# A pool mixer, a conv/LRU mixer and a PEER expert layer on one core: reordering the conditioning sums, the gating products and the transposes of the first norm

## The reference, cut to what matters

```
# first block: pool mixer (DEPTH = 1, so only this mixer runs)
h = x @ w_in;  u, z = h[:, :2048], h[:, 2048:]
per group g of 512 channels, window w = 2, 4, 8, 16:
    m[g] = moving_mean_w(u[g]) - u[g]
    m[g] = m[g] @ w_grp[g]
y = (m * scale * silu(z)) @ w_out
x = layer_norm(2**0.25 * x + y)
# second block, conditioned on c
ada = silu(c) @ w_ada + b_ada            # 6 * 1024 values: shift, scale, gate, twice
h = rmsnorm(x) * (1 + scale1) + shift1
z = h @ w_in2                            # gate_b, gate_c, xa, xr, gr
y = [gated short convolution ; gated linear recurrence], normalized per head
x = x + gate1 * (y @ w_out2)
h = rmsnorm(x) * (1 + scale2) + shift2
x = x + gate2 * peer(h)                  # per token 8 heads x 16 experts, gathered rows of 2 x 1024
out = rmsnorm(x) * final_g
```

## Time and profile before

| | |
|---|---|
| time, median of 3 runs | 1865.74 us (1862.46 to 1865.97) |
| time of the profiled execution | 1871.87 us |
| its span | 1870.0 us (1.9 us lie around the span) |
| TensorE busy / VectorE busy / ScalarE busy / POOL busy | 1598.8 / 1520.7 / 343.5 / 805.3 us |
| granted TensorE clock, mean of the span | 0.978 |
| HBM read | 621.06 MB |

### The profile page before, as it was taken

One profiled execution on the slowest core, in us unless ns is written; L12 is line 12 of the kernel. 1 busy time (PEld: TensorE's weight loads), 2 busy tenths in 40 slices (PEclk: granted clock), 3 DMA queues, 4 the chain that ended last, 5 costly groups with the idle time before them and its releaser, 6 DMA issues.

```text
span 1870.0 us, 19089 instructions
## 1 busy us (share of the span) xinstructions
PE 1598.8 (85%) x4856; PEld 830.0 (44%) x4856; DVE 1520.7 (81%) x3533; ACT 343.5 (18%) x955; POOL 805.3 (43%) x559
## 2 busy tenths in 40 slices
PE   7989999799988888888878888887888888788886
PEld 6768788677643333333333333332333333333332
DVE  5777786578768888888878888887888888788887
ACT  5223233254321101100111010011101001110101
POOL 1000000000016666666546666654666755456662
PEclk9999999899998999999999999999999999999999
DMA  8555463142229999999999999999999999999996
GB/s 304 180 203 179 168 229 144 40 175 85 90 77 391 421 421 421 421 422 421 422 404 412 422 418 422 422 410 383 413 422 422 422 421 416 387 416 421 422 422 255
DMA packets 93678, 623.89 MB, mean 334 GB/s; under 512 B 11440, under 2 KB 11440, under 8 KB 24240
## 3 DMA queue, kind: packets, MB, share of 16 engines
q0 software_dynamic: 78912, 570.46, 74.4%
q1 hardware_dynamic: 14704, 52.74, 7.7%
HBM read 621.06 MB, written 2.10 MB: 333 GB/s over the span
## 4 chain that ended last, share of the span: by engine, by line
DMA 41%; PE 30%; DVE 13%; issue 7%; POOL 5%; DVEq 3%; ACT 1%; POOLq 0%; ACTq 0%; SPq 0%
DMA arena<-in_experts,idx 38%; PE ps L625 9%; PE ps L413 5%; PE ps L414 5%; PE ps L415 5%; DVE arena L1336 5%; POOL arena L402 5%; PE ps L545 3%; DMA arena<-in_w_ada 2%; DVE arena L944 1%; DVE arena L1360 1%; PE ps L576 1%; DMA arena<-in_w_in 1%; DVE arena L1119 1%; DVE arena L1228 1%
## 5 line engine op out<-in xcount | busy, mean ns | idle before, releaser
L625 PE MATMUL ps<-arena 128*128 128x512 f32 x2048 | 1010.3, 623 | 225.3 <-DVE arena L1360 221.6
L402 POOL DMA_INDIRECT arena<-in_experts,idx x512 | 784.1, 1531 | 714.9 <-issue 389.3
L625 PEld LDWEIGHTS ps<-arena 128*128 128x128 f32 x2048 | 357.9, 192 | 829.4 <-DVE arena L1360 554.2
L1336 DVE CUSTOM_DVE_ANT_0 arena<-arena,ada 128x1024 f32<-128x1024 f32 x512 | 627.1, 1225 | 108.2 <-DMA arena<-in_experts,idx 89.9
L849 ACT ACTIVATE arena<-arena 128x1 f32<-128x1 f32 x512 | 103.9, 203 | 1135.1 <-DVE arena L1336 1135.1
L1360 DVE TENSOR_SCALAR arena<-ident,arena 128x128 f32<-128x128 f32 x512 | 171.0, 334 | 1.6 <-ACT arena L849 1.6
L365 POOL DMA_DIRECT2D arena<-in_w_ada x24 | 12.9, 538 | 247.4 <-DVE arena L944 237.3
L413 PE MATMUL ps<-xT_hl,w_hl 128*128 128x512 f32 x192 | 79.2, 412 | 9.4 <-DVE xT_hl L908 9.4
L903 DVE TENSOR_TENSOR w_hl<-arena,w_hl 128x1024 fp32r<-128x1024 f32 x47 | 57.4, 1221 | 30.0 <-ACT w_hl L653 29.9
L414 PE MATMUL ps<-xT_hl,w_hl 128*128 128x512 f32 x192 | 76.8, 400 | 0.0
L415 PE MATMUL ps<-xT_hl,w_hl 128*128 128x512 f32 x192 | 76.7, 400 | 0.0
(11 more groups left out here) (228 smaller groups left out, 1654.6 us busy)
## 6 DMA issues: line engine op xcount, KB each, us to landing
arena<-in_w_ada POOLq DMA_DIRECT2D x24, 1024.0 KB, 5.2
arena<-in_w_in SPq DMA_DIRECT2D x44, 512.0 KB, 3.3
arena<-in_experts,idx POOLq DMA_INDIRECT x512
arena<-in_w_out SPq DMA_DIRECT2D x14, 512.0 KB, 5.4
lnw<-in_w_in SPq DMA_DIRECT2D x8, 512.0 KB, 4.6
arena<-in_w_grp POOLq DMA_DIRECT2D x4, 1024.0 KB, 7.1
arena<-in_w_out SPq DMA_DIRECT2D x1, 4096.0 KB, 12.7
arena<-in_w_q SPq DMA_DIRECT2D x1, 4096.0 KB, 13.4
```

The source lines that it names most:

```text
L402: nc.gpsimd.indirect_dma_start(ring[:, n % RING, :], None, experts, bass.IndirectOffsetOnAxis(ap=idx[:, e, n:n + 1], axis=0)).then_inc(arr ...
L625: last = mm(ps[half][:, :], lhsT=diag[:, n % RING, :], rhs=ring[:, n % RING, DM + half * T:DM + (half + 1) * T], start=(e == 0 and n == 0) ...
L1336: nc.vector.tensor_tensor_reduce(out=urow, in0=urow, in1=h2cur, scale=1.0, scalar=0.0, op0=ALU.mult, op1=ALU.add, accum_out=dots[:, e, n:n ...
```

## The change

The sums over partitions of a group are taken inside the next group, after its second chunk (for the last group: after the second chunk of the output product). VectorE's order at a group's end becomes: one half, two gating products, one half, two gating products, remaining halves; in the last group all four gating products, then the remaining half. `ada_add` moves from the first to the third step of the next group (in the output product from chunks 0 and 1 to chunks 3 and 4). The transposes of h1 for tiles 0 and 1 are put between the first and the second chunk of the output tiles 2 and 3. The half blocks of the second mixer's first product go: the block is done once, for 512 tokens, and waits for the last tile's low parts in two steps.

```
@@ -414,16 +414,17 @@
                 mm(dst, lhsT=lhs[0], rhs=rhs[1], start=False, stop=False)
                 return mm(dst, lhsT=lhs[1], rhs=rhs[0], start=False, stop=final)
 
-            def chunk_mm(dst, w, x_hl, tok=slice(0, T), x_ready=None):
+            def chunk_mm(dst, w, x_hl, x_ready=None, halves=None):
 
                 for k in range(KD):
                     if x_ready is not None:
                         pe.wait_ge(x_ready, k + 1)
+                    if halves is not None and k % (KD // 2) == 0:
+                        pe.wait_ge(halves, 2 * NT - 1 + k // (KD // 2))
                     c = slice(k * P, (k + 1) * P)
-                    last = split_mm(dst[:, tok], (w[:, 0, c], w[:, 1, c]), (x_hl[:, k, 0, tok], x_hl[:, k, 1, tok]),
+                    last = split_mm(dst[:, :], (w[:, 0, c], w[:, 1, c]), (x_hl[:, k, 0, :], x_hl[:, k, 1, :]),
                                     k == 0, k == KD - 1)
-                if tok.stop == T:
-                    last.then_inc(w_mm, 1)
+                last.then_inc(w_mm, 1)
 
 
             pe.wait_ge(consts, 5)
@@ -434,6 +435,12 @@
                 pe.wait_ge(ada_acc, 2 * p + 2)
                 mm(ada_bank(p)[:, :], lhsT=ones[:, :], rhs=adaacc[:, p % ADA_ACC, :], start=True,
                    stop=True).then_inc(acc_mm, 1)
+
+            def sum_pairs(g):
+
+                for i in range(PAIRS[g]):
+                    pe.wait_ge(z_ready, GC * g + i + 1)
+                    sum_ada(PAIR0[g] + i)
 
             for g in range(NG):
                 for s in range(2 * GC):
@@ -445,6 +452,8 @@
                         if s - GC < PAIRS[g - 1]:
                             pe.wait_ge(ada_added, PAIR0[g - 1] + s - GC + 1)
                     chunk_mm(ps[s], hl_of(8 * g + s), xT_hl, x_ready=x_lo if g == 0 and s == 0 else None)
+                    if g and s == 1:
+                        sum_pairs(g - 1)
                 for d in range(GC):
                     for c in range(GC):
                         if d == 0:
@@ -453,9 +462,6 @@
                         last = split_mm(ps[d][:, :], (wgrp_hi[:, c, f], wgrp_lo[:, c, f]),
                                         (pooled_hi[:, c, :], pooled_lo[:, c, :]), c == 0, c == GC - 1)
                     last.then_inc(grp_mm, 1)
-                for i in range(PAIRS[g]):
-                    pe.wait_ge(z_ready, GC * g + i + 1)
-                    sum_ada(PAIR0[g] + i)
 
 
             def wout_mm(c, t, first, final):
@@ -483,12 +489,8 @@
                         pe.wait_ge(yin_ready, NKP - NT + t + 1)
                     last = wout_mm(c, t, c % 8 == 0, c == 7)
                 last.then_inc(w_mm, 1)
-            for t in range(NT):
-                for c in range(NWO - NRES, NWO):
-                    if t == 0:
-                        pe.wait_ge(lo_ready, NIN + c + 1)
-                    last = wout_mm(c, t, False, c == NWO - 1)
-                last.then_inc(yout_mm, 1)
+                if c == 1:
+                    sum_pairs(NG - 1)
 
             def transpose_h1(t):
                 pe.wait_ge(h1_ready, t + 1)
@@ -498,14 +500,15 @@
                                                h1tmp[:, t % 2, k * P:(k + 1) * P], ident[:, :])
                 last.then_inc(h1_tr, 1)
 
-            for t in range(NT - 1):
-                transpose_h1(t)
-
-            first = FIRST2
-            pe.wait_ge(h1_lo, 4)
-            for s in (XR, GR):
-                pe.wait_ge(lo_ready, first + s + 1)
-                chunk_mm(ps[s], hl_of(first + s), h1T_hl, slice(0, T // 2))
+            for t in range(NT):
+                for c in range(NWO - NRES, NWO):
+                    if t == 0:
+                        pe.wait_ge(lo_ready, NIN + c + 1)
+                    last = wout_mm(c, t, False, c == NWO - 1)
+                    if t >= 2 and c == NWO - NRES:
+                        transpose_h1(t - 2)
+                last.then_inc(yout_mm, 1)
+            transpose_h1(NT - 2)
             transpose_h1(NT - 1)
 
 
@@ -517,7 +520,6 @@
                 mm(ps[7][:, :], lhsT=headmean[:, :], rhs=(sqb if n % 2 == 0 else sqa)[:, 0:T],
                    start=True, stop=True).then_inc(norm_mm, 1)
 
-            pe.wait_ge(h1_lo, 2 * NT)
             read_by = {XR: xr_copied, GR: gg_ready, GCT: gc_copied, XA: v_ready, GB: ya_ready}
             for j in range(NJ):
                 for s in range(5):
@@ -525,7 +527,7 @@
                     pe.wait_ge(lo_ready, n + 1)
                     if j:
                         pe.wait_ge(read_by[s], j)
-                    chunk_mm(ps[s], hl_of(n), h1T_hl, slice(T // 2 if n < first + 2 else 0, T))
+                    chunk_mm(ps[s], hl_of(n), h1T_hl, halves=h1_lo if n == FIRST2 else None)
                     if j and s == XR:
                         head_means(2 * j - 2)
                     if j and s == GR:
@@ -728,12 +730,11 @@
                                    ps[4 * b + t][:, :].rearrange("p (k f) -> p k f", k=4)).then_inc(h1_hi, 1)
 
             for t in range(NT):
-                if t == NT - 1:
-                    h1_hi_part(0)
-                    h1_hi_part(1)
                 act.wait_ge(var_ready, t + 1)
                 nc.scalar.activation(stats[:, 13:14], stats[:, 13:14], ACT.Sqrt,
                                      bias=stats[:, 16:17]).then_inc(root_ready, 1)
+                if t >= 2:
+                    h1_hi_part(t - 2)
                 root_of_squares(xres[:, t, :], junk1, t + 1)
             for t in range(NT - 2, NT):
                 h1_hi_part(t)
@@ -1001,7 +1002,7 @@
                 b = 2 * PAIR0[g]
                 for s in range(GC):
                     lo_part(8 * g + s + 2)
-                    if s == 0 and g:
+                    if s == 2 and g:
                         for p in range(PAIR0[g - 1], PAIR0[g]):
                             ada_add(p)
                     if s:
@@ -1026,19 +1027,28 @@
                 if g == NG - 1:
                     for c in range(4):
                         yin_lo_part(c)
+                if g < NG - 1:
+                    ada_half(b)
+                    gated(g, 0)
+                    gated(g, 1)
+                    ada_half(b + 1)
+                    b += 2
+                    gated(g, 2)
+                    gated(g, 3)
+                else:
+                    for d in range(GC):
+                        gated(g, d)
                 while b < 2 * PAIR0[g + 1]:
                     ada_half(b)
                     b += 1
-                for d in range(GC):
-                    gated(g, d)
 
             for c in range(8):
                 lo_part(NIN + c + 2)
                 if c < 6:
                     yin_lo_part(2 * c + 4)
                     yin_lo_part(2 * c + 5)
-                if c < 2:
-                    ada_add(PAIR0[NG - 1] + c)
+                if c in (3, 4):
+                    ada_add(PAIR0[NG - 1] + c - 3)
                 if c < 4:
                     ada_half(2 * PAIR0[NG] + c)
             ada_add(NPAIR - 2)
@@ -1086,8 +1096,6 @@
                 nc.vector.bn_aggr(stats[:, 12:14],
                                   lnst[:, t, :].rearrange("p (a b) -> p a b", a=2)).then_inc(var_ready, 1)
                 dve.drain()
-                if t == NT - 1:
-                    h1_lo_part(0)
                 stt(row, row, stats[:, 12:13], lnw[:, 0, :], ALU.subtract, ALU.mult)
                 inverse_root(13, 2 * t + 1)
                 stt(row, row, stats[:, 13:14], lnw[:, 1, :], ALU.mult, ALU.add).then_inc(row_ready, 1)
@@ -1095,11 +1103,11 @@
                 if t >= 2:
                     dve.wait_ge(h1_tr, t - 1)
                 tt(h1, row, ada[:, 1, :], ALU.mult)
-                if t == NT - 1:
-                    h1_lo_part(1)
                 inverse_root(14, 2 * t + 2)
                 stt(h1, h1, stats[:, 14:15], ada[:, 0, :], ALU.mult, ALU.add).then_inc(h1_ready, 1)
-            for t in range(NT - 2, NT):
+                if t == 2:
+                    h1_lo_part(0)
+            for t in range(1, NT):
                 h1_lo_part(t)
```

29 lines of the change are left out of this document (12 added, 17 removed).

## The result

The changed kernel takes 1849.2 us (median of 4 runs, 1847.89 to 1849.7) against 1865.86 us before (median of 4): ratio 0.9904, 95% interval 0.989 to 0.9919. A later comparison with more runs gives 1849.34 against 1865.73, ratio 0.9911 (0.9897 to 0.9925). So 16.4 to 16.7 us are gained; 21.8 were forecast. The measured time lies inside the stated range (1839.5 to 1855) and 0.2 us above the forecast's own (1840 to 1849). The two profiled executions, 1871.87 and 1847.89 us, lie 24.0 us apart, 7 us more than the medians. Where these 7 us come from is the main question of the experiments.

The account below looks back on a forecast made before the run. The gather fills the DMA engines from 560 us on; before it TensorE paces, so the gain is an earlier gather start. 1.0 + 8.1 + 7.7 + 5.0 = 21.8 us off the 1865.74 median gives about 1844.0 us; range 1839.5 to 1855.

Parts of the forecast that it names:

- Part 1: Ends of the first three groups: TensorE's waits and restarts go, gaining 1.0, 8.1 and 7.7 us.
- the gain does not depend on that: The profiled execution lay 6.1 us over the median; the full 21.8 us was therefore taken off the median too.
- rival A: VectorE falls behind in the third and fourth groups and output product: 12 us of gain lost, 1856 us; chance 0.12.
- B: The first norm gives nothing, its first two blocks perhaps all at the lower clock: 1851 us; chance 0.16.
- Do the waits only move?: Group ends: waits do not reappear in the next group; slack 4.0 us in the second, 3 us in the third; cost nothing.
- Part 2: First norm, up to the gate matmuls: transposes inside tiles 2 and 3 and whole blocks bring these 5.0 us forward.
- C: Sums inside the next group: a half over 4 us late holds the group and starts it cold; some 1879 us; chance 0.03.
- D: Start of the gather: set by the mixer's loads or the ScalarE chain, so no change, about 1865 us; chance 0.04.

Follow-up runs that it names:

- first profile of before: The kernel before the change, unchanged, as first profiled: profiled execution 1871.87 us, median of runs 1865.86 us.
- second profile: A repeat profile of an unchanged kernel: the kernel before took 1866.59 us (median), the changed kernel 1849.34 us.
- norm part: Only the norm edits (transposes inside output tiles 2 and 3, whole blocks), against the kernel before: 1860.24 us, ratio 0.9971.

## Why the prediction was right, and where its sum was off

- **Part 1, the groups.** The mechanism is right in each point: banks 0 and 1 gated before the product ends, sums at full speed inside the next group, no wait for a sum or a bank anywhere (ten sums run after second chunks; the prediction counted eight, those of the groups). The term is oversized. It was 16.8 us; against the first profile of before the last sums moved by 16.5 us, but in that execution the clock had fallen at both ends, in the second profile at the third group's end alone. Against the second it is 11.0 to 11.5 us, and by the runs 9.9. The step that failed is the sentence that "the gain does not depend on that": the profiled execution lay 6.1 us over the median, and 5.1 of these were in the group ends, which the change removes. Priced from the second profile by the same count, the three ends give an estimate of 0.8 + 3.9 + 7.0 = 11.7 us instead of 16.8 (6.3 and 9.4 less 2.4 each, and 1.0 less the 0.2 by which the first group's wait was shorter); that alone is the 5.1 us between forecast and result. The other differences are small: 1.8 us less by the runs than by this count, 0.8 more in the norm, and 0.7 to 1.0 that both parts together give over their sum. That the time still lies in the stated range is owed to the width that the rivals A and B gave it: it is 0.2 us outside the forecast's own range.
- **Do the waits only move?** No, as forecast. The slack was 6.7 and 4.8 us instead of 4.0 and 3 in the first profile, since the last load but one was in by 119.9 instead of 122.6. In the second profile the same load came at 122.2, and the slack was 4.7 and 6.0 us: the 4.0 was a fair figure, and the landing decides it. Of the last load's 7.55 us, which the prediction read as its length, 3.9 were spent behind the load before it.
- **VectorE falls behind (rival A).** It did not: no wait for it in the third or fourth group. Only with 9.2 us of added work does a part of this appear.
- **Part 2, the norm.** 5.0 forecast, 5.6 to 5.7 by the profiles (93.4 to 87.7, or 93.1 to 87.5 for the part alone), 5.8 by the runs. The fourth row was complete at 335.37 + 1.29 = 336.7; the forecast 353.5, shifted by the 16.5 us of the groups, is 337.0. The block ran at the lower clock for 4.0 us instead of the 5.3 assumed.
- **Rivals B, C and D.** B did not come; half of its premise did (the block begins at the lower clock), and filling the idle time shows what that costs: some 2 us. C's mechanism was produced by added work and gives waits of the size worked out, but no kernel slower than before (its price, by its own terms, is 1878, not 1879). D is out: the gate matmuls moved by 16 to 22 us and the end with them.

What stays open: why the same loads in flight together cost a load 6.5 us in one execution and 8.4 in another, and when a wait of about 3 us takes the clock down. Both were seen, neither was tried by itself.

## What to carry to other kernels

If the profiled execution is slower than the median, its surplus sits somewhere: it may sit in the very wait that the change removes, and then the gain of the median is smaller by it. Take a second profile, or count such a wait with its clock loss at less than the profile shows. Where one late producer holds two consumers (here the sums and the gating), opening one lock alone can cost time, since what used to run in the shadow of the stop is laid bare; look at all waits on the same producer before moving one.

## What was not expected of the hardware

- The clock is not a fixed price of a wait: behind 3.53 us at L435 it stayed full, behind 4.89 us matmuls were at half speed until 6.0 us after the restart, and behind 2.80 us (norm part only) the mean grant from 122 to 138 was 0.89. It fell around 2.61 and 3.40 us too and stayed full behind 2.34.
- It also fell while TensorE was at work: with 26 matmuls filling the idle time, 1.5 us into a dense block, behind two pauses of 1.0 and 2.0 us. With the pauses filled as well it stayed at 1.00.
- A load of 1 MB issued with nothing else in flight lands in 4.9 to 5.3 us (94 of 95). Behind one such load and beside a weight chunk it takes 6.5 to 8.6 us, and this differs from execution to execution of one kernel: 6.5 and 8.4 us in the two profiles of the changed kernel.
